# A three-layer mixture-of-experts kernel: experts with 65 to 96 tokens get a 32-slot second block, begun behind the pair's own gate and up products

## The reference

```
for e in range(16):
    he = jax.nn.silu(t @ w_gate[e]) * (t @ w_up[e])      # t: 256 x 1024, w_gate, w_up: 1024 x 512
    y = y + combine[:, e:e + 1] * (he @ w_down[e])       # w_down: 512 x 1024
```

## Time and profile before

| | |
|---|---|
| median of 3 runs | 1488.08 us (1482.8 to 1489.64) |
| profiled execution | 1482.8 us, span 1480.9 us |
| TensorE matmul busy | 1320.8 us, 89% of the span |
| VectorE, ScalarE busy | 581.3 us, 431.7 us |
| granted TensorE clock, mean | 0.968 |
| read from HBM | 445.38 MB |

### The profile page before, as it was taken

How to read it: one execution, slowest core, us unless ns; L and a number is a source line. 1 busy time by engine, 2 the same in 40 slices (tenths; PEclk the granted TensorE clock), 3 DMA queues, 4 the chain that set the end, 5 groups by cost and what they waited for, 6 DMA issues and landing times.

```text
span 1480.9 us, 20887 instructions
## 1 busy us (share of the span) xinstructions
PE 1320.8 (89%) x7694; PEld 815.7 (55%) x7695; DVE 581.3 (39%) x1234; ACT 431.7 (29%) x693; POOL 410.2 (28%) x190
## 2 busy tenths in 40 slices
PE   7999987889899889998789799789997979889975
PEld 6886775534334389766234334279886853333422
DVE  5598543612112162447214222279007062322224
ACT  4554433211111146443111111145435331111110
POOL 5892643100000067151000000069964710000000
PEclk9999999999999999999899999999999999999998
DMA  7664566999999975518589999976544479999953
GB/s 285 215 201 173 186 228 231 393 402 426 426 428 428 391 283 183 190 58 338 231 344 420 426 422 428 397 269 235 191 150 191 170 321 412 422 416 420 427 221 126
DMA packets 89628, 448.04 MB, mean 303 GB/s; under 512 B 7804, under 2 KB 9768, under 8 KB 70952
## 3 DMA queue, kind: packets, MB, share of 16 engines
q1 hardware_dynamic: 85856, 445.87, 75.4%
q10 hardware_dynamic: 3656, 0.57, 0.3%
HBM read 445.38 MB, written 1.05 MB: 301 GB/s over the span
## 4 chain that ended last, share of the span: by engine, by line
PE 65%; DMA 15%; DVE 9%; issue 4%; POOL 3%; ACT 3%; ACTq 0%; SPq 0%; DVEq 0%; POOLq 0%
PE ps L419 63%; DMA ring_hi<-in_moe_w_up 10%; DMA ring_hi<-in_w_up 3%; POOL WLO L2528 3%; DMA ring_hi<-in_ada_w 1%; ACT WHI L1326 1%; DVE Z L1944 1%; DVE Z L1932 1%; DVE Z L1945 1%; DVE Z L1943 1%; DMA ring_lo<-in_w_ckv 1%; PE ps L884 1%; DMA ring_lo<-in_ret_w_in 1%; DMA ring_lo<-in_w_out 1%; POOL RS L2497 1%
## 5 line engine op out<-in xcount | busy, mean ns | idle before, releaser
L2528 POOL TENSOR_TENSOR WLO<-ring_lo,WHI 128x1024 fp32r<-128x1024 f32 (+1 forms) x154 | 379.3, 2485 | 702.6 <-ACT WHI L1326 700.7
L419 PE MATMUL ps<-ring_hi,Z 128*64 128x512 f32 x1248 | 375.4, 616 | 25.3 <-DMA ring_hi<-in_moe_w_up 14.4
L419 PE MATMUL ps<-ring_lo,Z 128*64 128x512 f32 x1152 | 350.6, 613 | 33.6 <-issue 24.3
L419 PEld LDWEIGHTS ps<-ring_lo,Z 128*64 128x64 f32 x1152 | 111.0, 141 | 248.2 <-issue 234.1
L1326 ACT ACTIVATE WHI<-ring_lo 128x1024 fp32r<-128x1024 f32 (+1 forms) x160 | 165.5, 1048 | 214.1 <-PE ps L419 177.3
L419 PEld LDWEIGHTS ps<-ring_hi,Z 128*64 128x64 f32 x1248 | 119.6, 142 | 153.7 <-issue 147.5
L2195 DVE TENSOR_TENSOR Z<-ps,Z 64x512 f32<-64x512 f32 x48 | 33.1, 689 | 357.4 <-ACT Z L1533 354.2
L1533 ACT ACTIVATE Z<-ps 64x512 f32<-64x512 f32 x48 | 28.4, 591 | 370.4 <-PE ps L419 357.6
L419 PE MATMUL ps<-WHI,HTH 128*128 128x512 f32 x320 | 126.8, 396 | 7.2 <-POOL WLO L2528 3.2
L419 PE MATMUL ps<-WLO,HTH 128*128 128x512 f32 x320 | 125.1, 391 | 0.0
L419 PE MATMUL ps<-WHI,HTL 128*128 128x512 f32 x320 | 125.1, 391 | 0.0
(11 more groups left out here) (299 smaller groups left out, 1719.2 us busy)
## 6 DMA issues: line engine op xcount, KB each, us to landing
ring_lo<-in_ada_w SPq DMA_DIRECT2D x22, 2048.0 KB, 8.1
ring_lo<-in_moe_w_gate SPq DMA_DIRECT2D x16, 2048.0 KB, 12.1
ring_lo<-in_moe_w_up SPq DMA_DIRECT2D x16, 2048.0 KB, 16.5
ring_lo<-in_moe_w_down SPq DMA_DIRECT2D x16, 2048.0 KB, 12.6
ring_hi<-in_moe_w_gate SPq DMA_DIRECT2D x16, 2048.0 KB, 13.6
ring_hi<-in_moe_w_up SPq DMA_DIRECT2D x16, 2048.0 KB, 18.5
ring_hi<-in_moe_w_down SPq DMA_DIRECT2D x16, 2048.0 KB, 16.9
ring_lo<-in_ret_w_in SPq DMA_DIRECT2D x12, 2048.0 KB, 8.1
```

Source lines behind the costliest of these rows:

```text
L419: return nc.tensor.matmul(o, l, r, start=start, stop=stop, skip_group_check=True)
L2528: nc.gpsimd.tensor_tensor(WLO[:, q, 0:size], slot(r)[:, q * size:(q + 1) * size], WHI[:, q, 0:size].bitcast(F32), ALU.subtract).then_inc(S ...
```

## The change

- The table gets new rows. An expert with 65 to 96 tokens "fits": it has one block of 32 slots and no 64-slot block. One with more than 96 tokens goes through the 64-slot blocks as before. The table also counts the fitting experts before each one.
- `early` is new, called for both experts of every pair right behind the pair's gate and up products: two table loads, a branch, and for a fitting expert the gather of 32 slots with features on partitions (32 matmuls of 32 columns from the high and low parts of the rows), gain and shift by VectorE, and gate and up with four 32-row strips side by side (32 matmuls of 256 columns). Behind it, in every pair, TensorE loads one more integer and waits for `f_h`, the hidden rows of all fitting experts so far.
- `late` is new, called for both experts behind the down products and ahead of `more`: two table loads, a branch, and for a fitting expert the turned selection and weights, the turned hidden rows, the down product in four strips, and the scatter.
- `more` stays behind `late`, with its own loads and branch. Its selection is made inside its loop; `choose_more` in every pair goes, and VectorE makes the 32-slot selection of the next pair's experts instead (`choose_fits`, two 128x256 operations), behind `more`.
- ScalarE and VectorE get the matching `early` and `late`. VectorE loads eight integers a pair in place of four; SyncE loads one more per expert and waits for `f_gu` and `f_y` as well. TensorE's wait for the table moves from ahead of the first pair to behind its gate and up products. The semaphores of the 64-slot blocks no longer exist once for each layer.

The core of it:

```diff
+            def early(p, k, a, wg, wu, first):
+
+                e = 2 * p + a
+                fits = pe.value_load(TBL[32 * L:32 * L + 1, 3, bass.ds(e, 1)], min_val=0, max_val=1)
+                c1 = pe.value_load(TBL[32 * L:32 * L + 1, 4, bass.ds(e, 1)], min_val=1, max_val=48)
+                bank = (B_XG, B_TR)[a]
+                with pe.If(fits > 0):
+                    if k == 1:
+                        wait_moe(pe, L, "swt", p + 1)
+                        wait_moe(pe, L, "ws", p + 1)
+                    if first and L:
+                        pe.wait_ge(S("gate_in"), L)
+                    wait_moe(pe, L, "self", e + 1)
+                    for c in range(KC):
+                        for t in range(NT):
+                            for x in (XHR, XLR):
+                                ins = mm(ps[:, bank, STRIP * c:STRIP * c + STRIP], x[t][:, P * c:P * c + P], SELF[:, a, t, 0:STRIP],
+                                         t == 0 and x is XHR, t == NT - 1 and x is XLR)
+                    ins.then_inc(S("f_xg"), 1)
+                    pe.wait_ge(S("f_xe"), c1)
+                    for c in range(KC):
+                        for r, w in enumerate((wg, wg, wu, wu)):
+                            ins = mm(ps[STRIP * r:STRIP * r + STRIP, bank, 0:256], XEF[:, c, :], w[:, c, 256 * (r % 2):256 * (r % 2) + 256], c == 0, c == KC - 1)
+                    ins.then_inc(S("f_gu"), 1)
+
+            def late(p, k, a, wd, final):
+
+                e = 2 * p + a
+                fits = pe.value_load(TBL[32 * L:32 * L + 1, 3, bass.ds(e, 1)], min_val=0, max_val=1)
+                c1 = pe.value_load(TBL[32 * L:32 * L + 1, 4, bass.ds(e, 1)], min_val=1, max_val=48)
+                bank = (B_XG, B_TR)[a]
+                with pe.If(fits > 0):
+                    if k == 0:
+                        wait_moe(pe, L, "swt", p + 2)
+                        wait_moe(pe, L, "ws", p + 2)
+                    elif not final:
+                        wait_moe(pe, L, "xe_a", p + 2)
+                        wait_moe(pe, L, "xe_v", p + 2)
+                    for t in range(NT):
+                        mm(ps[:, bank, P + P * t:2 * P + P * t], SELF[:, a, t, :], TURNER[:, t, 0:P], True, True)
+                    by4 = SGF[a].rearrange("p (i c) -> p c i", c=4)
+                    for c in range(4):
+                        for r in range(2):
+                            mm(ps[CAP * r:CAP * r + CAP, bank, STRIP * c:STRIP * c + STRIP], by4[:, c, :],
+                               CST[CAP:P, C_ID + CAP + STRIP * r:C_ID + CAP + STRIP * r + STRIP], True, True)
+                    for t in range(NT):
+                        ins = mm(ps[:, bank, 3 * P:3 * P + 32], SELF[:, a, t, :], TURNER[:, t, P:P + 32], t == 0, t == NT - 1)
+                    ins.then_inc(S("f_tp"), 1)
+                    pe.wait_ge(S("f_ht"), c1)
+                    for c in range(4):
+                        for r in range(4):
+                            ins = mm(ps[STRIP * r:STRIP * r + STRIP, bank, 0:256], HTF[:, c, :], wd[:, c, 256 * r:256 * r + 256], c == 0, c == 3)
+                    ins.then_inc(S("f_y"), 1)
+                    pe.wait_ge(S("f_ye"), c1)
+                    scatter_more()
...
+                if first:
+                    pe.wait_ge(S("table"), L + 1)
+                for a in range(2):
+                    early(p, k, a, wg[a], wu[a], first)
+                pe.wait_ge(S("f_h"), pe.value_load(TBL[32 * L:32 * L + 1, 5, bass.ds(2 * p + 1, 1)], min_val=1, max_val=48))
...
                 for a in range(2):
+                    late(p, k, a, wd[a], final)
+                for a in range(2):
                     more(p, k, a, wg[a], wu[a], wd[a], final)
...
-                        pe.wait_ge(m(L, "x_sel"), b1 + 2 * p + 1 + j)
+                        pe.wait_ge(m(L, "x_sel"), b1 + j)
...
-            pe.wait_ge(S("table"), L + 1)
...
+                fits_done[a] = sp.value_load(TBL[32 * L:32 * L + 1, 5, bass.ds(e, 1)], min_val=1, max_val=48)
+            sp.wait_ge(S("f_gu" if j < 2 else "f_y"), fits_done[a])
...
+            def choose_fits(e, a):
+
+                V.tensor_tensor(SELF[:, a].rearrange("p t (k s) -> p t k s", s=STRIP), bc(slots[:, 0:STRIP], [NT, P // STRIP, STRIP], 1, 1),
+                                RANKF[:, :, bass.ds(e, 1)].unsqueeze(3).broadcast_to([P, NT, P // STRIP, STRIP]), ALU.is_equal).then_inc(S("moe_self"), 1)
+
+            def early(a, fits, c1):
+
+                bank = (B_XG, B_TR)[a]
+                with dve.If(fits > 0):
+                    dve.wait_ge(S("f_xg"), c1)
+                    for c in range(KC):
+                        o = ps[:, bank, STRIP * c:STRIP * c + STRIP]
+                        if shift is None:
+                            ins = V.tensor_scalar(XEF[:, c, :], o, gain[:, c:c + 1], None, ALU.mult)
+                        else:
+                            ins = V.tensor_scalar(XEF[:, c, :], o, gain[:, c:c + 1], shift[:, c:c + 1], ALU.mult, ALU.add)
+                    ins.then_inc(S("f_xe"), 1)
+                    dve.wait_ge(S("f_sg"), c1)
+                    V.tensor_tensor(SGF[a], ps[CAP:P, bank, 0:256], SGF[a], ALU.mult).then_inc(S("f_h"), 1)
...
-                load = [[dve.value_load(TBL[0:1, L, i, bass.ds(e + a, 1)], min_val=i, max_val=(3, 48)[i]) for i in range(2)] for a in range(2)]
+                load = [[dve.value_load(TBL[32 * L:32 * L + 1, i, bass.ds(e + a, 1)], min_val=i % 3, max_val=(3, 48, 0, 1, 48)[i]) for i in (0, 1, 3, 4)] for a in range(2)]
...
-                for a in range(2):
-                    choose_more(e + a, a, 0, load[0][1] + (e + a))
...
+                if not final:
+                    for a in range(2):
+                        choose_fits(e + 2 + a, a)
...
+            for b, over in enumerate((CAP, CAP + STRIP, 2 * CAP, 3 * CAP)):
+                ins = V.tensor_scalar(TBF[0:1, 1 + b, :], TBF[0:1, 0, :], over + 0.5, None, ALU.is_gt)
...
+            V.tensor_tensor(TBF[0:1, 5, :], TBF[0:1, 1, :], TBF[0:1, 2, :], ALU.subtract)
...
+            V.tensor_copy(TBL[32 * L:32 * L + 1, 2, :], TBF[0:1, 8, :])
+            V.tensor_copy(TBL[32 * L:32 * L + 1, 5, :], TBF[0:1, 9, :])
+            V.tensor_copy(TBL[32 * L:32 * L + 1, 0, :], TBF[0:1, 7, :])
+            V.tensor_copy(TBL[32 * L:32 * L + 1, 3, :], TBF[0:1, 5, :])
+            V.tensor_tensor(TBL[32 * L:32 * L + 1, 1, :], TBF[0:1, 8, :], TBF[0:1, 7, :], ALU.subtract)
+            V.tensor_tensor(TBL[32 * L:32 * L + 1, 4, :], TBF[0:1, 9, :], TBF[0:1, 5, :], ALU.subtract).then_inc(S("table"), 1)
```

More of the change, by code:

```diff
@@ L1556, in pair @@
                 silu(p, k, 1)
+                if first:
+                    act.wait_ge(S("table"), L + 1)
+                for a in range(2):
+                    early(p, a)
                 if k == 0:
@@ L2217, in pair @@
                 e = 2 * p
-                load = [[dve.value_load(TBL[0:1, L, i, bass.ds(e + a, 1)], min_val=i, max_val=(3, 48)[i]) for i in range(2)] for a in range(2)]
-                hidden(p, k, 0)
-                if first and L:
-                    dve.wait_ge(S("gate_in"), L)
+                if first:
+                    hidden(p, k, 0)
+                    if L:
+                        dve.wait_ge(S("gate_in"), L)
+                load = [[dve.value_load(TBL[32 * L:32 * L + 1, i, bass.ds(e + a, 1)], min_val=i % 3, max_val=(3, 48, 0, 1, 48)[i]) for i in (0, 1, 3, 4)] for a in range(2)]
+                if not first:
+                    hidden(p, k, 0)
                 hidden(p, k, 1)
+                for a in range(2):
+                    early(a, *load[a][2:])
                 if k == 0:
@@ L2236, in pair @@
                 for a in range(2):
-                    more(e + a, a, *load[a])
+                    late(e + a, a, *load[a][2:])
+                for a in range(2):
+                    more(e + a, a, *load[a][:2])
+                if not final:
+                    for a in range(2):
+                        choose_fits(e + 2 + a, a)
             def choose_next(q):
```

131 lines of the change are left out of this document (102 added, 29 removed).

## The result

The changed kernel takes 1695.62 us (median of 4 runs, 1692.52 to 1698.64), the kernel before 1486.13 us on the same chip: ratio 1.1409, 95% interval 1.1373 to 1.1446. The profiled execution has a span of 1693.5 us against 1480.9, so 212.6 us are to be explained. Its page first: span, busy time, the clock and DMA in 40 slices, the instruction queues, the chain, the costliest matmuls.

A forecast was written before the change was run, and what follows sets the result against it. TensorE's own stream bounds nearly everywhere, weights taking over for a few us. Profiled 1482.8 us + 170 (loads, branches, code) - 17 (blocks) + 7 (table) = 1643, with 5 for the median 1648 us; range 1495 to 1705.

The forecast's parts named there:

- the main term: Loads, branches and skipped code in all 24 expert pairs on TensorE: 7.1 us a pair, 170 us slower.
- Code, loads and branches: TensorE's added table loads, branches and jumps over unfetched code, less waits it had anyway: 7.1 us a pair, 170 us.
- Price of a packet: Fetching one 256-instruction packet behind a jump on TensorE: 5.2 us, between 4 and 6 in the ends kept.
- Number of packets: TensorE's instruction queue: about 1.6 times as many packets, a pair's code growing from 2.4 to 5.1 packets.
- rival 1: Changed loop's code stays loaded, so 6 of 24 pairs have no code waits: 36 us less, 1612 us; chance 0.1.
- The second jump waits, not the first: In TensorE's pairs the packet behind the first boundary is there; the second jump always waits for the next one.
- Branches of 3 to 6 us in most pairs: Expected sign: TensorE branches this long behind gate and up as well as behind the down products.
- Heads: Table loads and branch before each conditional body, 1.7 us each; 2.4 us a pair show behind the down products.
- rival 2: No code waits come on top, only loads and branches count: 1.1 us a pair, 26 us, 1504 us; chance 0.1.
- Blocks: Two experts leave 64-slot blocks, 53.6 us, for 32-slot paths of 18.5 us each: 17 us saved, between 0 and 25.
- Table: Ahead of each layer's first pair, more small VectorE operations delay TensorE 2.3 us: 7 us over three layers, 0 to 8.
- Rival 3: Weights set every pair's pace, hiding loads and jumps, so the change is faster: about 1465 us; chance 0.12.

The follow-up runs named there:

- j_code: Kernel before, with 162 already-met waits added inside each of a pair's two skipped whole-block bodies on TensorE, no head added: 1615.6 us.
- o_far: Changed kernel with every instruction kept, TensorE's skipped early, late and whole-block bodies laid behind the end of its program: 1509.2 us.
- n_nobody: Changed kernel with the 32-slot path's test made empty, so both experts over 64 tokens take whole 64-slot blocks; skipped code stays: 1705.9 us.
- m_hint: Changed kernel with two tests a pair on TensorE (early; late with whole blocks), each jump announced ahead to instruction fetch, bodies in place: 1507.0 us.
- h_heads: As n_nobody, with TensorE's early and late bodies replaced by one wait each, loads, compares and branches kept: 1567.1 us.
- q_far: Kernel before with only TensorE's whole-block bodies laid behind the end of its program: 1481.2 us.
- q_hint: Kernel before with one test round both whole-block bodies of a pair on TensorE, the jump announced at the pair's start: 1477.4 us.
- l_unroll: Changed kernel with TensorE's loop over the two middle quads written out, so no branch back: 1655.5 us.
- u_hint: m_hint with TensorE's loop over the two middle quads written out as well: 1511.0 us.
- m_near: Changed kernel with TensorE testing once a pair for both early, both late and both whole-block bodies, all left in place: 1622.8 us.

## Why the prediction was right, and where its terms were off

The sum gave 1648 us with 1495 to 1705 as its range, and 1580 to 1700 for the forecast alone; it is 1695.6. The mechanism stands: j_code makes such a loss from skipped code alone, o_far takes 186 of 209 us away by laying the code elsewhere. That the main term came out so close is in part luck, as its parts show.

- **Code, loads and branches.** Forecast 170 us. The windows of the layers grew by 211.6 us, with the 10 us that the 32-slot path gives back (n_nobody) by 222. Of these 54 are TensorE's lower clock (o_far against the changed kernel, same matmuls). The other 168 are idle time, the forecast's 170. But the parts are off and cancel: the forecast had 2.4 us a pair, 58 in all, for heads, 6.0, 144, for late code over what before had, and 1.3, 31, off for other waits. Idle time at "issue" grew by 39 us in loads, register operations and short branches, by 87 in branches of over 1 us and by 42 in stretches without an instruction, 128 for the last two; other waits gave back some 10. The step that failed is what the sum left out: it priced idle time as itself, and it costs a third more (54 on 157), since the matmuls behind it run at 1.2 GHz for some us. These 54 us are the 48 by which the time was missed.
- **Price of a packet.** 5.2 us from jump to landing, with 4 and 6 as its ends. The branches that wait at line 940 took 4.0 to 4.6 us, so it was somewhat high. j_code's 4.4 us (129 us for 29 packets, clock included) is another measure, which the changed kernel has at 2.5. A count of packets would mislead altogether: m_hint fetches 143 and loses 20 us.
- **Number of packets.** Forecast 1.6 times; 79 became 161, 2.04 times. The forecast was at odds with itself here: 5.1 packets in all 24 pairs, where before fetched 2.4 in 18 of them, are 79 more, so 2.0 times, and 1.6 is what rival 1 would give. Rows 13 had shown that before's loop code is not fetched again; the changed loop's is (nine packets from 436 to 509 us, its second pass in the first layer). That was left open, and rival 1 is out: the second pass pays too, and the three branches back, 21.5 us together, are dearer than other jumps.
- **The second jump waits, not the first.** Held behind gate and up, where all 13 waits are at the pair's second jump. Behind the down products late's two jumps never wait (435 ns at most); 8 of the 14 waits are at the third of the four jumps, 6 at the fourth. "Branches of 3 to 6 us in most pairs" held narrowly (14 of 24 pairs, but 2 of 8 in the first layer), "issue" near 200 us (194.0) and a DMA share below 0.85 (0.84, 0.74, 0.71) too. No whole block is gathered by rows any more, and VectorE's eight pieces of 128x32 came twice.
- **Heads.** 1.1 us a pair as rival 2 has them; o_far's 19 distances grew by 16 us, 0.8 each. The size was near, but it is no separate term. Heads with before's bodies in place (h_heads) cost 80 us, not 26: loads and branches come on top of late fetches in the same lead (4.4 us at the one place where rows 8 and 9 show it), the slower TensorE no longer waits for weights in their stead (4.2 us for 22.7), and the clock is lower.
- **Blocks.** Forecast -17 us. TensorE's timeline of the changed kernel through the second layer's:

```profile
782.57 5.09 PE L428 MATMUL ps<-ring_hi,Z 128*32 128x256 f32 x64 [1.94 <-DVE Z L2268]
788.62 0.68 PE L428 MATMUL ps<-TURN,SELQ 128*128 128x160 f32 x4 [0.97 <-DVE Z L2271]
...
797.54 0.44 PE L428 MATMUL ps<-TURN,SELF 128*128 128x128 f32 x2
...
801.81 2.94 PE L428 MATMUL ps<-ring_hi,Z 128*32 128x256 f32 x32 [2.42 <-ACT Z L1671]
808.01 0.80 PE L428 MATMUL ps<-YHS,SELTS 64*128 64x512 f32 x2 [3.27 <-DVE YLS L2297]
...
814.02 9.86 PE L428 MATMUL ps<-ring_lo,Z 128*64 128x512 f32 x32 [3.93 <-issue]
```

  Early lasts from 776.02 to 788.62, 12.6 us for the forecast's 9.9; late from 797.54 to 810.09, 12.6 for 8.6. The gather of 32 columns (part of it at the lower clock) took 4.6 us, not 2.5, gate and up 5.1, not 4, and the three copies kept TensorE 2.4 us, not 1.2; the waits of 1.94 and 3.27 us were right. So 25.2 us where 26.4 went: the half-width block saves about 1 us of path by itself. n_nobody's 10 us must then come from what lies round it; that was not taken apart. (In what bounds the kernel, the forecast read 86% as the lowest share of matmuls in a layer; rows 1 give 88%, 230.17 of 261.9 us. The sum does not use it.)
- **Table.** Forecast +7 us. VectorE goes from the first `choose_fits` to its first chunk in 3.6 us (284.50 to 288.09) where it took 2.2, but the first silu of the first layer comes at 294.4 instead of 296.5, and the stretches between the layers' pairs are not longer (208.4 and 283.7 us from last to first silu, 209.6 and 285.1 before). This term was nothing, as far as such stretches can tell: in q_far, where nothing there was changed, the first is 205.8 us.
- **Rival 3** (weights set the pace) is out for the changed kernel: weights ended one wait of 4.4 us in the second layer. But q_far and q_hint, with 45.5 and 43.4 us of such waits, show where it takes over, some 3 to 10 us below before.

The last two mistakes cancel: -17 and +7 were about -10 and 0. In the Trainium skill, Runtime: NRT & Kernel Launch, section Instruction fetch mechanics, the rule that a taken branch outside the window stalls agrees with these jumps (o_far's fall-through at 69 ns, its two taken jumps at up to 6.0 us), and so does its room for 2048 instructions with the loop that is fetched again. The same section of the Trainium skill prefers code written out to loops for this reason; l_unroll's 40 us agree, u_hint, no faster than m_hint (1511.0 for 1507.0 us), doesn't. What stays open: why a body's exact place decides which pair pays (l_unroll, u_hint), what the announcement is worth without the fewer tests, and what n_nobody's 10 us are made of.

## What to carry to other kernels

A conditional body that is nearly never run is not free on an engine whose sequencer is fed in order: count its instructions in every place where it is jumped over. Ask once for several cases, announce the jump or lay the body out of the way, and look at the lead of the sequencer over the matmuls before adding even a cheap head: once the lead is spent, loads and branches count at full price. A late fetch that costs nothing while TensorE would wait for weights instead begins to cost as soon as something else makes TensorE slower. Price an idle stretch of TensorE above its length, since the clock behind it is lower.

## What the runs showed of the hardware that I had not expected

- A failed test that falls through costs 69 ns on TensorE; a taken one mostly 0.2 to 0.4 us where it does not wait. Where it waits, it takes 1.1 to 4.7 us forward in the changed kernel, 4.0 to 4.6 at line 940, and up to 6.5 in m_near.
- A taken branch back over a loop whose code is fetched again is dearer than one forward: 6.3 to 7.8 us against 4.7 at most in the same kernel, and 4.7 at most with a quarter of the weight traffic.
- The sequencer also stands still where there is no branch: 3.7 us between a table load and the next register operation at 537.9 us of the changed kernel, with one instruction packet in that time.
- After 4.31 us of idleness the first 5 us of work ran at a clock of 0.50 (1.2 GHz); over the kernel such stretches made the same 7848 matmuls 54 us longer than in o_far.
- With the jumps announced, m_hint had few late first jumps (2 of 24 over 1 us, 1.4 at most) but half of the second ones, announced directly behind the first, were late (12 of 24 over 1 us, up to 6.6). With the loop written out (u_hint) 7 of the first jumps were late too, up to 6.3 us: an announcement is no guarantee.
